# Cache pages and key expansion handed over turned as well as by rows, in a latent-attention decode

## The reference

```python
def mla_expand(lat, w_kvb, g_kn):
    kv = jnp.einsum('nkc,che->nkhe', lat[..., :KV_LORA], w_kvb.reshape(KV_LORA, MLA_HEADS, QK_NOPE + V_DIM))
    return rms_norm(kv[..., :QK_NOPE], g_kn), kv[..., QK_NOPE:], lat[..., KV_LORA:]

def mla_decode(q_nope, q_pe, lat_new, cache, page_table, w_kvb, g_kn):
    def page_part(phys):
        k_nope, v, kpe = mla_expand(cache[phys], w_kvb, g_kn)
        sc = mla_scores(q_nope, q_pe, k_nope, kpe)
        m = sc.max(axis=-1)
        e = jnp.exp(sc - m[..., None])
        return m, e.sum(axis=-1), jnp.einsum('nhsk,nkhd->nhsd', e, v)
    m_p, l_p, a_p = lax.map(page_part, page_table.T)
    ...  # the 8 new rows likewise, causally, then one softmax over all
```

## Time and profile before

| | |
|---|---|
| median of 3 runs (lowest, highest) | 2223.14 us (2217.63, 2225.77) |
| profiled execution, its own time | 2224.36 us |
| its span | 2222.5 us |
| mean granted TensorE clock | 0.944 |
| TensorE, VectorE, ScalarE busy | 91%, 52%, 37% of the span |
| the page loop's products (line 1592) | from 1637.2 to 1908.6 us of the span |

### The profile page before, as it was taken

How to read it: one execution, slowest core, us unless ns; L and a number is a source line. 1 busy time by engine, 2 the same in 40 slices (tenths; PEclk the granted TensorE clock), 3 DMA queues, 4 the chain that set the end, 5 groups by cost and what they waited for, 6 DMA issues and landing times.

```text
span 2222.5 us, 33644 instructions
## 1 busy us (share of the span) xinstructions
PE 2011.6 (91%) x13396; PEld 1720.5 (77%) x13396; DVE 1146.5 (52%) x1942; ACT 813.9 (37%) x1605; POOL 31.4 (1%) x57
## 2 busy tenths in 40 slices
PE   4797899999998877999977999988789999889997
PEld 1684799979986554999965999863568888669997
DVE  1462754458834434654357554467735555356532
ACT  1420443335433323443224443232435445235422
POOL 0000000000010000000000000000000000000000
PEclk9899999999997999999998999997789999799999
DMA  6774665554450997565664665632007677434442
GB/s 233 262 264 150 227 212 209 192 206 133 130 169 5 266 272 249 185 209 193 231 217 151 210 209 199 225 107 88 0 24 256 209 247 245 161 113 145 148 148 79
DMA packets 229511, 398.82 MB, mean 179 GB/s; under 512 B 9288, under 2 KB 195567, under 8 KB 215793
## 3 DMA queue, kind: packets, MB, share of 16 engines
q1 hardware_dynamic: 224912, 332.69, 45.2%
q0 software_dynamic: 3296, 59.76, 8.1%
q10 hardware_dynamic: 1161, 4.34, 0.6%
HBM read 391.23 MB, written 59.76 MB: 203 GB/s over the span
## 4 chain that ended last, share of the span: by engine, by line
PE 81%; DVE 9%; DMA 3%; ACT 3%; issue 2%; ACTq 0%; SPq 0%; POOL 0%; DVEq 0%; POOLq 0%
PE bank L1164 38%; PE bank L1070 11%; PE bank L1592 8%; PE bank L1083 4%; PE bank L1035 3%; PE bank L1139 3%; PE bank L1251 2%; DVE rstd L1846 2%; PE bank L1392 1%; DMA work<-in_ada_w 1%; PE bank L1622 1%; PE bank L1129 1%; PE bank L1296 1%; PE bank L1344 1%; PE bank L1308 1%
## 5 line engine op out<-in xcount | busy, mean ns | idle before, releaser
L1713 DVE TENSOR_TENSOR ring_lo<-ring,ring_hi 128x1024 fp32r<-128x1024 f32 (+1 forms) x324 | 380.1, 1213 | 365.3 <-ACT ring_hi L695 365.2
L695 ACT ACTIVATE ring_hi<-ring 128x1024 fp32r<-128x1024 f32 (+1 forms) x324 | 323.1, 1046 | 333.8 <-PE bank L1164 279.6
L1164 PE MATMUL bank<-hidden_hi,ring_hi 128*128 128x320 f32 x1024 | 318.9, 311 | 0.0
L1164 PE MATMUL bank<-hidden_hi,ring_lo 128*128 128x320 f32 x1024 | 316.4, 309 | 0.0
L1164 PE MATMUL bank<-hidden_lo,ring_hi 128*128 128x320 f32 x1024 | 316.3, 309 | 0.0
L1164 PE MATMUL bank<-h_hi,ring_hi 128*128 128x320 f32 x896 | 279.6, 312 | 0.1
L1164 PE MATMUL bank<-h_lo,ring_hi 128*128 128x320 f32 x896 | 276.2, 308 | 0.0
L1164 PE MATMUL bank<-h_hi,ring_lo 128*128 128x320 f32 x896 | 275.9, 308 | 0.0
L1164 PEld LDWEIGHTS bank<-hidden_hi,ring_hi 128*128 128x128 f32 x1024 | 192.2, 188 | 20.1 <-issue 20.1
L1164 PEld LDWEIGHTS bank<-hidden_lo,ring_hi 128*128 128x128 f32 x1024 | 192.3, 188 | 0.0
L1164 PEld LDWEIGHTS bank<-hidden_hi,ring_lo 128*128 128x128 f32 x1024 | 192.2, 188 | 0.0
(11 more groups left out here) (281 smaller groups left out, 3334.4 us busy)
## 6 DMA issues: line engine op xcount, KB each, us to landing
ring<-in_mlp_w SPq DMA_DIRECT2D x128, 1024.0 KB, 5.4
work<-in_ada_w SPq DMA_DIRECT2D x88, 1024.0 KB, 7.5
ring<-in_swa_w_qkv SPq DMA_DIRECT2D x18, 1024.0 KB, 5.0
out_swa_s<-in_state_swa POOLq DMA_DIRECT2D x8, 2016.0 KB, 9.7
ring<-in_conv_w_in SPq DMA_DIRECT2D x12, 1024.0 KB, 5.9
work<-in_state_swa SPq DMA_DIRECT2D x48, 256.0 KB, 8.8
work<-in_cache_mla SPq DMA_DIRECT2D x64, 160.0 KB, 2.2
ring<-in_ada_w SPq DMA_DIRECT2D x8, 1024.0 KB, 11.9
```

The lines of the kernel that those rows point to most:

```text
L695: act.activation(ring_hi[:, place, part], ring[:, s, part], ACT.Copy).then_inc(sem("weights_hi"), 1)
L1164: mm = pe.matmul(bank[a % 4][:, 0:T], w[:, k, :], x(k), start=first and k == 0 and j == 0, stop=last and k == KD - 1 and j == 2)
L1713: dve.tensor_tensor(ring_lo[:, s, part], ring[:, s, part], ring_hi[:, place, part], ALU.subtract)\
```

## The change

Some inputs are handed to the kernel in a second layout: the cache's latents by rows and turned, its rope keys turned, the key weights turned. The kernel loads what it had turned. The new latents leave turned and are put in order outside. On TensorE no turn is left in the page loop, and two of the nine latent turns ahead of it. `lT_parts` holds four pages in place of eight. SP loads a sequence's turned pages and rope keys as soon as the products of the sequence two before are done, and its rows, as before, behind the value products. ScalarE waits for the pages. The scores of the new rows go behind the fifth page's products. `layouts` and `assemble` run on the host, outside the time.

```diff
-            pages(0, 0)
-            sp.wait_ge(sem("mla_prompt_done"), 1)
-            pages(1, 1)
-            with sp.Fori(1, NS // 2) as i:
-                for half in range(2):
-                    sp.wait_ge(sem("md_pv"), 2 * i + half - 1)
-                    pages(2 * i + half, half)
+            for n in range(NS):
+                if n == 1:
+                    sp.wait_ge(sem("mla_prompt_done"), 1)
+                if n >= 2:
+                    sp.wait_ge(sem("md_latents_split"), PAGES * (n - 1))
+                    sp.wait_ge(sem("md_keys"), PAGES * (n - 1) + 1)
+                turned_pages(n)
+                if n >= 2:
+                    sp.wait_ge(sem("md_pv"), n - 1)
+                page_rows(n)
...
+            act.dma_start(ml_wkT, A["key_expansion_turned"]).then_inc(sem("kvb_landed"), 16)
...
-            for t in range(3):
-                rows = P if t < 2 else TS
-                act.wait_ge(sem("latent_turned"), t + 1)
-                act.activation(ml_tok[0:rows, t, :], bank[4 + t % 2][0:rows, 0:LAT], ACT.Copy).then_inc(sem("latent_tok"), 1)
+            act.wait_ge(sem("latent_turned"), 1)
+            act.activation(ml_tok[0:TS, 0:LORA], bank[4][0:TS, 0:LORA], ACT.Copy).then_inc(sem("latent_tok"), 1)
...
-            for h in range(H):
-                act.wait_ge(sem("wk_turned"), h + 1)
-                act.activation(ml_wkT[:, h, :], bank[6 + h % 2][:, 0:LORA], ACT.Copy).then_inc(sem("wk_copied"), 1)
...
-                act.wait_ge(sem("md_turned"), PAGES * n + j + 1)
-                ins = act.activation(lT_parts[0][:, :, j, :], bank[6][:, 0:2 * P].rearrange("p (c k) -> p c k", c=2), ACT.Copy)
+                if j in (0, 4):
+                    act.wait_ge(sem(f"pages_{'last' if j else 'first'}_landed{half}"), 128 * (n // 2 + 1))
+                if k >= 4:
+                    act.wait_ge(sem("md_keys"), k - 2)
+                act.activation(lT_parts[0][:, :, k % 4, :], md_lT[half][:, j, :, :], ACT.Copy).then_inc(sem("md_latents"), 1)
...
-            for hd in range(H):
-                if hd >= 2:
-                    pe.wait_ge(sem("wk_copied"), hd - 1)
-                turn(bank[6 + hd % 2][:, 0:P], ml_kvb[:, 0, hd, 0:NOPE], P)
-                turn(bank[6 + hd % 2][:, P:2 * P], ml_kvb[:, 1, hd, 0:NOPE], P).then_inc(sem("wk_turned"), 1)
...
+                if j == 4:
+                    for c in range(2):
+                        pe.matmul(bank[6][0:TS, 384:448], ml_lat[:, c, TP:T], md_q[:, c, n, :, :].rearrange("p h s -> p (h s)"),
+                                  start=c == 0, stop=c == 1)
+                    mm = pe.matmul(bank[6][0:TS, 448:512], ml_rope[:, TP:T], md_qr[:, n, 0, :], start=True, stop=True)
...
+                pe.wait_ge(sem(f"page_rows_landed{n % 2}"), 16 * PAGES * (n // 2 + 1))
...
-            page_turn(0, 0)
             for k in range(NS * PAGES):
                 n, j = divmod(k, PAGES)
-                if k + 1 < NS * PAGES:
-                    page_turn(*divmod(k + 1, PAGES))
                 page_products(n, j, {3: page_spread, 4: page_values, 5: page_total, 6: page_result}.get(j) if n else None)
```

More of the change, by code:

```diff
@@ L550, in _, with page_number @@
             sp.wait_ge(sem("unit_done"), UNIT0["mla_qb"])
-            def pages(n, half):
+            def page_number(n, j):
+                return sp.value_load(pages_sb[0:1, n * PAGES + j:n * PAGES + j + 1], min_val=0, max_val=N_PHYS - 1)
+            def turned_pages(n):
+                half = n % 2
                 for j in range(PAGES):
-                    phys = sp.value_load(pages_sb[0:1, bass.ds(n * PAGES + j, 1)], min_val=0, max_val=N_PHYS - 1)
-                    sp.dma_start(md_pg[half][:, j, 1:PG], A["cache_mla"][0, bass.ds(phys, 1)].rearrange("a p e -> (a p) e"))\
-                      .then_inc(sem(f"pages_{'first' if j < 4 else 'last'}_landed{half}"), 16)
-            pages(0, 0)
-            sp.wait_ge(sem("mla_prompt_done"), 1)
-            pages(1, 1)
-            with sp.Fori(1, NS // 2) as i:
-                for half in range(2):
-                    sp.wait_ge(sem("md_pv"), 2 * i + half - 1)
-                    pages(2 * i + half, half)
+                    phys, landed_here = page_number(n, j), sem(f"pages_{'first' if j < 4 else 'last'}_landed{half}")
[5 more added lines that the diff above has]
+            def page_rows(n):
+                for j in range(PAGES):
+                    phys = page_number(n, j)
[11 more added lines that the diff above has]
+                page_rows(n)
             mlp(3)
@@ L1487, in _ @@
             pe.wait_ge(sem("rope_done"), 1)
[L1488 to L1495, removed]
+            for c in range(2):
+                mm = turn(bank[4][0:TS, c * P:(c + 1) * P], ml_lat[:, c, TP:T], P)
+            mm.then_inc(sem("latent_turned"), 1)
+            pe.wait_ge(sem("kvb_landed"), 32)
             for i in range(4):
@@ L1557, in _ @@
             pairings = ((0, 0), (0, 1), (1, 0))
[L1559 to L1577, removed]
             def page_products(n, j, middle):
@@ L1624, in page_values @@
                     if b == 1:
-                        pe.matmul(own[:, AT_VALUES], new, ml_tok[0:TS, 2, 0:LORA], start=False, stop=False)
+                        pe.matmul(own[:, AT_VALUES], new, ml_tok[0:TS, 0:LORA], start=False, stop=False)
                         pe.matmul(own[:, 0:1], new, ones[0:TS, 0:1], start=False, stop=False)
@@ L2266, with layouts, assemble @@
            ("swa2_p", (1, 1, 256, 2, H, SWA_HD)), ("swa2_s", (1, NS, 1032, 2, H, SWA_HD)),
-           ("pool_p", (1, 1, HIST, D)), ("pool_s", (1, NS, HIST, D)), ("mla_p", (1, 1, TP, LAT)), ("mla_s", (1, NS, SS, LAT))]
+           ("pool_p", (1, 1, HIST, D)), ("pool_s", (1, NS, HIST, D)), ("latents_turned", (P, 2, T)), ("ropes_turned", (ROPE, T))]
+def layouts(inputs):
+    pages = np.asarray(inputs["cache_mla"])[0]
+    turned = pages[:, :, 0:LORA].reshape(N_PHYS, PAGE, 2, P).transpose(0, 3, 2, 1)
+    w_kvb = np.asarray(inputs["mla_w_kvb"])[0].reshape(LORA, H, NOPE + VD)
+    return {"pages_rows": pages[:, :, 0:LORA], "pages_turned": turned, "pages_rope": pages[:, :, LORA:].transpose(0, 2, 1),
+            "key_expansion_turned": w_kvb[:, :, 0:NOPE].transpose(2, 1, 0)}
+def assemble(out):
+    y = {name: np.asarray(out[f"out_{name}"]) for name, _ in OUTPUTS}
+    latents = np.concatenate([y.pop("latents_turned").transpose(2, 1, 0).reshape(T, LORA), y.pop("ropes_turned").T], axis=1)
+    return (*y.values(), latents[0:TP].reshape(1, 1, TP, LAT), latents[TP:].reshape(1, NS, SS, LAT))
 def kernel(**inputs):
@@ L2275 @@
     arrays = {name: np.ascontiguousarray(inputs[name]) for name in INPUTS}
+    arrays |= {name: np.ascontiguousarray(a) for name, a in layouts(inputs).items()}
     arrays["tables"] = tables()
```

50 lines of the change are left out of this document (26 added, 24 removed).

## The result

| | before | after |
|---|---|---|
| median (lowest, highest) of 18 runs each | 2222.7 us (2217.6, 2228.5) | 2209.8 us (2196.2, 2221.3) |
| ratio of the times | | 0.993, interval [0.991, 0.995] |
| profiled execution, its span | 2224.4, 2222.5 us | 2196.2, 2194.3 us |
| loop, first to last product | 271.3 us | 254.1 us |

A forecast was written before the change was run, and what follows sets the result against it. TensorE's own work was taken as the bound, 81% of the span. Gains of 31.7 (page loop), 1.9 (loop's start) and 2.8 (before the attention) sum to 36.4 us, giving 2187 us as a median, range 2177 to 2203.

The forecast's parts named there:

- Cost: from nothing to the case below: Page loads in the loop: SP's 24 issues take 27.9 us a sequence, under 30.3; cost from nothing to a rival's.
- By about 25 us into the sequence the field is clear: Page loop: GpSimd's copies, up to 23.2 us to land, are done before ScalarE wants the first turned page at 24 to 25.
- The third rival: Page loop: turned loads stay behind GpSimd's copies, first pages land at 30 us; 1 to 2 us for six sequences, 2197; chance 0.10.
- The fourth rival: Page loop: DMA engines become the bound, copies and loads served one after the other, 39.9 us a sequence, 2244; chance 0.05.
- The page loop, 31.7: Decode loop: turns removed and part of the maxima wait gone, 34.4 to 30.3 us a sequence; 31.7 us gained in all.
- the first rival: Page loop: turns cost more than the gaps they leave, 1.0 us more a sequence, loop 8 more, 2179; chance 0.10.
- The maxima: Page loop: VectorE's chain and TensorE's need for the maxima meet at 9.3 us; 0.2 us a sequence of old wait gone.
- the second rival: Page loop: the maxima become the bound, TensorE waits some 1 us more a sequence, 8 us, 2195; chance 0.13.
- The loop's start, 1.9: From VectorE's flag to the loop's first product: 2.5 us sooner, about half lost if the clock rises as before; 1.9 taken.
- Before the attention, 2.8: Ahead of the attention: nine latent turns become two, 1.5 us; VectorE's wait for the weights' high parts goes, 1.3.
- the forecast's 36.4: Whole kernel: total gain in us, 31.7 from the loop, 1.9 from its start, 2.8 before the attention.

The follow-up runs named there:

- the two edited forms of the kernel before: Kernel before with half of GpSimd's window copies out of the loop, 2223.8 us; kernel before with only the edits ahead of the loop, 2221.3 us.
- the two groups: All 28 runs of the unedited changed kernel: 13 from 2196 to 2204 us (median 2199.8), 15 from 2208 to 2221 us (median 2214.7).

## Why the prediction was wrong

**The step that failed** is the cost of the page loads: "Cost: from nothing to the case below". It set 24 issues at 27.9 us against 30.3 and took it that issues go on at SP's pace while loads wait. They do not: beside a copy the queue is held behind eight to twelve loads, and a sequence's issues so lose 10 to 12 us. The issues themselves were estimated too dear (23 us, not 27.9), but the sum of both, 34 to 35 us, is over TensorE's 29.8.

- *"By about 25 us into the sequence the field is clear"*: right for the copy, but SP's rows, which come behind the blocked turned loads, end at 1685.5, 33.6 us into it, and the next sequence's loads run into the next copy.
- *The third rival* named the place, turned loads behind copies, and ScalarE's wait with squares behind it. Its size failed: 1 to 2 us for each of six sequences. The delay is not paid in each sequence; it adds up at 4 to 5 us until the last loads of a sequence fall behind the start of the next copy, and is then paid at once, 19 us, with 6 of them at a lower clock.
- *The fourth rival*, the DMA engines as the bound, did not come: 0.87 to 0.93 of their time was in use without a wait for pages.
- *The page loop, 31.7*: by the kernel with half of the copies moved, first to last product is 236.3 us for 271.3, so 35.0. A sequence gives 4.6, not 4.1. The odd page's turn was read as 0.14 us, from its start; with the rope product ahead of it the pair took 1772.06 to 1772.42, 0.36, and the rope product alone takes 0.14 now (1789.12 to 1789.26). So a turn cost 0.22, four times a sequence 0.3 more: the first rival's mechanism, at a third of its size. The other 0.2 was not traced.
- *The maxima*: the two meet, as counted; the second rival did not come.
- *The loop's start, 1.9*: from the flag to the first product 3.16 us before, 0.76 now (1623.63 to 1624.39), 2.4. The clock did not hold the gain back: the loop's first 5 us ran at a granted 0.72 (1624.39 to 1629.39), where the earlier trace rows has 0.51.
- *Before the attention, 2.8*: 2.2 from latent turns, as against 1.5; VectorE's wait is gone, but the lower clock in the attention takes its 1.3 back before the flag.

The three gains make 35.0 + 2.4 + 2.2 = 39.6 us; what follows the last product is 1.5 to 1.9 us longer than before (315.4 and 315.8 us against 313.9). Runs differ by as much without the change: the two edited forms of the kernel before take 315.1 and 315.5 there. With it taken off, 38 us are gained where nothing waits for pages, near the forecast's 36.4. The waits take 17.8 (254.1 - 236.3) or about 31.5 (267.9 in the mean) of it: 2222.7 - 38 + 17.8 = 2202 and 2216, against medians of 2200 and 2215 of the two groups. The kernel with half of the copies moved is 5 us faster than this sum gives (2185). In its profile these 5 us lie ahead of the loop: its first product starts at 1627.2, where 2.2 and 2.4 off the 1637.3 before would give 1632.7. The kernel before with its copies moved starts at 1631.5 itself, so this part differs by as much between runs; why stays open.

## What to carry to other kernels

Before a transfer is moved or split, add up for its queue what each issue takes and how long the queue stands when loads pile up; a deficit of a few us a round is hidden by the lead of the buffers and then paid at once. Read the packets of each queue as well as its bytes. Look at what else moves at the moment of issue, not only at landing times from a quieter moment. A copy that nobody waits for belongs where the DMA engines stand still, or in short packets.

## What the runs showed of the hardware

- A load of 128 KB that landed 2 us after its issue alone took up to 21.3 us beside a copy of long packets from another queue, 12.0 at the longest beside the same bytes in pieces with a fifth of the packet length. In 9 us in which the loads and the copy of long packets both waited, the two queues moved 46 packets each, 0.05 MB and 3.01.
- SP's queue took twelve loads beside a copy (six of 128 KB, six of 32) and then held the thirteenth for 7.5 us; at another copy it held the ninth, behind eight of 128 KB, for 10.1. So it is not a fixed number of loads; what is counted was not tried.
- Taking 16 transposes from an otherwise idle stretch left TensorE 7.4 us idle, and the attention behind it ran at a granted 0.50 for its first 20 us, where it had been 0.56; two heads of it took 11.04 us for 8.36.
